# Moving the fourth gate step of each feed-forward's first chunk ahead of half of the operand building

## What is computed

```python
def rmsnorm(x, g):
    y = xf * lax.rsqrt(jnp.mean(xf * xf, axis=-1, keepdims=True) + EPS)
    return (y * g.astype(jnp.float32)).astype(x.dtype)

def swiglu(h, w_in, w_out):
    a, b = jnp.split(h @ w_in, 2, axis=-1)
    return (jax.nn.silu(a) * b) @ w_out
...
x = x + 0.5 * swiglu(rmsnorm(x, norm_ffn1[l]), ffn1_w_in[l], ffn1_w_out[l])
m, k, v, lf, s_fin = token_mix(...)
x = x + m
x = x + 0.5 * swiglu(rmsnorm(x, norm_ffn2[l]), ffn2_w_in[l], ffn2_w_out[l])
```

## Time and profile before

| | |
|---|---|
| median of 3 runs | 1251.35 us |
| the profiled execution, device time | 1252.58 us |
| its span | 1250.7 us |
| PE busy | 1210.6 us, 97% |
| DVE busy | 819.7 us, 66% |
| ACT busy | 572.0 us, 46% |
| POOL busy | 106.0 us, 8% |
| mean granted clock of TensorE | 0.994 |
| w_out loads of the first chunks, issue to landing | 2.9 us for 256 KB |

### The profile page before, as it was taken

The page is one execution under the profiler, slowest core; times in us unless marked ns, Lnnn a source line. Parts: engine busy times, 40 slices in busy tenths (PEclk is TensorE's granted clock), DMA queues, the critical chain, the costliest instruction groups (busy, mean ns, idle before and its releaser), DMA issues.

```text
span 1250.7 us, 29938 instructions
## 1 busy us (share of the span) xinstructions
PE 1210.6 (97%) x12005; PEld 1129.6 (90%) x12005; DVE 819.7 (66%) x1557; ACT 572.0 (46%) x1047; POOL 106.0 (8%) x247
## 2 busy tenths in 40 slices
PE   9999999999999999998978999999999999999998
PEld 8999999999999999996656666599989999999998
DVE  6799848838956423336756566654679839847954
ACT  6454424514534211535866776743345424524534
POOL 1000000000005000000222522214000000000000
PEclk9999999999999999999989999999999999999999
DMA  8133333233324343344798999723123332333322
GB/s 208 39 96 102 110 93 102 85 101 85 94 93 129 107 135 92 107 170 154 245 366 301 347 353 343 241 69 95 58 84 102 92 111 80 93 99 102 93 77 72
DMA packets 187145, 172.79 MB, mean 138 GB/s; under 512 B 11890, under 2 KB 149651, under 8 KB 187027
## 3 DMA queue, kind: packets, MB, share of 16 engines
q1 hardware_dynamic: 185858, 167.47, 42.5%
q0 software_dynamic: 1104, 3.67, 0.8%
q10 hardware_dynamic: 64, 0.02, 0.0%
HBM read 162.19 MB, written 8.93 MB: 137 GB/s over the span
## 4 chain that ended last, share of the span: by engine, by line
PE 82%; DVE 9%; issue 3%; ACT 3%; DMA 2%; SPq 0%; ACTq 0%; DVEq 0%; POOLq 0%
PE ps L2221 40%; PE ps L2359 28%; PE ps L1038 2%; PE ps L1123 2%; PE ps L1138 2%; PE ps L963 1%; DVE z_lo L2849 1%; PE ps L1003 1%; DMA d_keys<-in_cache_k 1%; PE ps L983 1%; DVE b_lo L2818 1%; PE ps L801 1%; ACT d_keysT L1383 1%; DVE z_sum L2826 0%; DMA d_log_f<-in_cache_logf,page_ids 0%
## 5 line engine op out<-in xcount | busy, mean ns | idle before, releaser
L2359 PE MATMUL ps<-b_lo,z_hi 128*128 128x272 f32 x1008 | 292.1, 290 | 0.0
L2359 PE MATMUL ps<-b_hi,z_hi 128*128 128x272 f32 x1008 | 290.8, 288 | 1.0 <-ACT z_kept L2566 1.0
L2359 PE MATMUL ps<-b_hi,z_lo 128*128 128x272 f32 x1008 | 290.9, 289 | 0.0
L2491 ACT ACTIVATE w_hi<-w_raw 128x2048 fp32r<-128x2048 f32 (+2 forms) x56 | 90.0, 1608 | 234.2 <-PE ps L2221 234.2
L2359 PEld LDWEIGHTS ps<-b_hi,z_hi 128*128 128x128 f32 x1008 | 190.0, 188 | 1.4 <-issue 1.4
L2359 PEld LDWEIGHTS ps<-b_hi,z_lo 128*128 128x128 f32 x1008 | 189.7, 188 | 0.0
L2359 PEld LDWEIGHTS ps<-b_lo,z_hi 128*128 128x128 f32 x1008 | 189.3, 188 | 0.0
L2221 PE MATMUL ps<-g_hi,w_hi 128*128 128x272 f32 x704 | 148.6, 290 | 6.6 <-DVE g_lo L2794 3.5
L2221 PE MATMUL ps<-n_hi,w_hi 128*128 128x272 f32 x704 | 148.9, 289 | 1.9 <-issue 1.0
L2221 PE MATMUL ps<-n_hi,w_lo 128*128 128x272 f32 x704 | 148.3, 288 | 0.0
L2221 PE MATMUL ps<-g_hi,w_lo 128*128 128x272 f32 x704 | 148.2, 289 | 0.0
(11 more groups left out here) (398 smaller groups left out, 1952.1 us busy)
## 6 DMA issues: line engine op xcount, KB each, us to landing
w_raw<-in_ffn_w_in SPq DMA_DIRECT2D x87, 512.0 KB, 5.0
d_keys<-in_cache_k SPq DMA_DIRECT2D x128, 256.0 KB, 5.3
d_values<-in_cache_v SPq DMA_DIRECT2D x124, 256.0 KB, 6.2
w_raw<-in_ffn_w_out SPq DMA_DIRECT2D x48, 384.0 KB, 3.6
w_raw<-in_w_in_mix SPq DMA_DIRECT2D x28, 512.0 KB, 4.8
w_raw<-in_ffn_w_out SPq DMA_DIRECT2D x16, 256.0 KB, 2.9
w_raw<-in_w_out_mix SPq DMA_DIRECT2D x8, 512.0 KB, 4.7
suffix_scratch<-d_log_f_sums SPq DMA_DIRECT2D x32, 64.0 KB, 2.1
```

The source lines that it names most:

```text
L2359: mm = pe.matmul(bank(out), w[j][:, a, k * P:(k + 1) * P], x, start=(k == 0 and n_pass == 0 and not more), stop=(k == KB - 1 and n_pass == ...
L2491: nc.scalar.activation(w_hi[j][:, 0:kt * UC], w_raw[j][:, 0:kt * UC], ACT.Copy).then_inc(w_hi_ready, 1)
```

## The change

The changed kernel has three edits. The first is in DVE's list of the first chunk: the building of B21 and B22 is cut in two halves of two instructions, and the fourth gate step stands between them. The second is in that gate step alone: the low part of A1's weight is written after `g_lo` and not before `ffn_gated`. The third is in PE's output units: the last two K tiles are taken one after the other, each with a wait of its own.

```diff
@@ unit
                 if x_wait is not None:
-                    order = [(t, k) for ks in (range(kt - 2), range(kt - 2, kt)) for t in range(2) for k in ks]
+                    order = [(t, k) for ks in (range(kt - 2), (kt - 2,), (kt - 1,)) for t in range(2) for k in ks]
@@ g_wait
-                        if k == 0 or k == kt - 2:
-                            pe.wait_ge(g_ready, done - 2 if k == 0 else done)
+                        if k == 0 or k >= kt - 2:
+                            pe.wait_ge(g_ready, done - 2 if k == 0 else done - (kt - 1 - k))
@@ gate_step of the vector block
-            def gate_step(pair, j, q, f, tile, next_kt, stage=None):
+            def gate_step(pair, j, q, f, tile, next_kt, stage=None, late_split=False):
...
-                split_lo(pair + 1, j, next_kt)
+                if not late_split:
+                    split_lo(pair + 1, j, next_kt)
...
                 nc.vector.tensor_tensor(lo, g_f[:, :, :], hi.bitcast(F32), ALU.subtract).then_inc(g_ready, 1)
+                if late_split:
+                    split_lo(pair + 1, j, next_kt)
@@ ffn of the vector block
                         gate_step(p0 + 1, 0, q0 + 2, f, 2, kt)
-                        build_full(f, norm, range(KB, KD))
-                        gate_step(p0 + 1, 1, q0 + 3, f, 3, kt)
+                        build_full(f, norm, range(KB, KB + 2))
+                        gate_step(p0 + 1, 1, q0 + 3, f, 3, kt, late_split=True)
+                        build_full(f, norm, range(KB + 2, KD))
                         build_sum(f, U1, b_full(f, B11), b_12[:, :, :], ALU.subtract)
```

## The result

The changed kernel is slower. In two comparisons, each against runs of the kernel before on the same chips, it took 1263.09 us (6 runs, 1258.26 to 1265.84) and 1261.02 us (6 runs, 1258.69 to 1265.35). The ratios are 1.0084 with a 95% interval of 1.0064 to 1.0103, and 1.0067 with 1.0045 to 1.0089, so it is 8 to 11 us slower. Forecast were 6.4 us and at most 9. The direction, the place and the length of DVE's list were right. The price of the slow clock was put too low, 3.0 us where it took 3.9 to 4.7 in two traces, and a third place, the last chunk of the first feed-forward, was not in the sum.

The account below looks back on a forecast made before the run. The prediction took DVE's list between `g_lo` and B0's low part as the bound: 1252.58 + 3.4 (list) + 3.0 (clock) = 1259.0 us against the profiled execution, median 1257.7, range 1254.0 to 1260.5.

Parts of the forecast that it names:

- What bounds the kernel: Ahead of B0, DVE's list from `g_lo` to the weight's low part sets its start; 0.26 us slack in first feed-forward.
- What edits 1 and 2 win: In the fourth gate step `g_lo` starts 0.92 us sooner in the first feed-forward, 0.71 in the second.
- What they cost: On DVE, `g_lo` to first sum grows from 0.64 to 3.27 us; sums start 1.71 and 1.92 us later.
- Edit 3 at nothing, and the stalls gathered into one: Added K tile waits cost nothing; PE's stall leaves A0, giving one gap of about 5 us ahead of B0 per feed-forward.
- Sum without the clock: At DVE's addition behind B0: +1.47 us in the first feed-forward, +1.92 in the second, together +3.4.
- The clock: During B0 the clock falls after both gathered gaps, 1.5 us each, +3.0; bounds nothing to 4.6 us each.
- In the later chunks ... PE does not stand at the last K tiles, so the order there changes nothing: In later chunks and first units with `x_in`, the new K tile order changes no time.
- the sign that all behind B0's addition would be later by one constant amount: Expected in the trace if right: everything from B0's addition on shifts later by one constant amount.
- the queue alone: DVE's list slips 3.4 us, clock holds or falls at one gap: 1254.7, or 1256.2 with one fall; chance 0.27.
- the exchange: Three instructions fit where DVE would wait anyway, the stall moves from A0 to B0: 1251.3; chance 0.04.
- the faster case: B0's low part does not decide B0's start, A0's stalls and slow clock are won, 5.0 us: 1246.3; chance 0.03.
- the slower case: Both gaps make the clock low for longer, 2.5 to 4.6 us each: 1259.7 to 1263.9; chance 0.08.

Follow-up runs that it names:

- the run with the gap filled: Changed kernel plus 36 matmuls with unread results at the end of A1 in both first chunks, output loop written out: 1256.51 us, ratio 1.0019.
- the run with the page sums late: Changed kernel with DVE's sums over the gathered values moved behind A1's weight in the first feed-forward's last chunk: 1260.07 us, ratio 1.0067.
- the run that had 0.2 and 0.4 us of list and lost 4.4: Changed kernel without the first edit, all four builds ahead of the fourth gate step again: 1256.82 us, ratio 1.0035.

## Why the prediction was wrong, point by point

- *What bounds the kernel:* right. In the changed kernel B0's low part set B0's start in both feed-forwards (before, PE ran from A0's gap into the first B0 without a pause, by the small slack that the prediction names); a longer list lost time, a shorter one won it.
- *What edits 1 and 2 win:* right, 0.9 and 0.7 us at `g_lo`. In the first feed-forward it starts 3.1 us after `ffn_a` (68.49 - 65.34) where it took 3.8 (69.17 - 65.33), and `ffn_a` itself waits for PE now and not for the builds; in the second the same 3.8 became 3.1.
- *What they cost:* right. 3.28 us from `g_lo` to the first sum against 3.27.
- *Edit 3 at nothing, and the stalls gathered into one:* the gap was forecast at about 5 us and measured at 5.15 and 4.94. That gathering has no price of its own was wrong: the run with edit 3 alone is 1.0023 of before.
- *Sum without the clock:* right. +3.4; 3.0 in the run with the gap filled, 3.4 with B0 started 0.34 us behind its low part as the sum has it.
- *The clock:* the step that failed. "I take a fall at both, 1.5 us each" carried the size of a fall after a gap of 1.88 us over to gaps of 5 us. The falls came at both. But of the six gaps of 4.94 to 5.15 us (the two traces and that of the run with the page sums late) five were followed by a low level of 6.8 us that began inside the gap, and one by 3.4 us. In the first trace B0 took 2.1 and 2.6 us longer, in the second 1.4 and 2.5: 4.7 and 3.9 us where the sum had 3.0. The case of longer falls, "2.5 to 4.6 us each", was named and given only 0.08.
- *"In the later chunks ... PE does not stand at the last K tiles, so the order there changes nothing":* true of the K tiles. But the gap at the gather was there before the change, its length varies from execution to execution, and I did not put it into the range. In the first trace that stretch carries 4.1 of 13.1 us. With it fell the sign that all behind B0's addition would be later by one constant amount.
- With 3.4 for the list, 3.9 to 4.7 for the clock and 0.2 for the first B0's later start the sum is 7.5 to 8.3 us, which is the second comparison (8.4 us by its ratio). The first, with 10.5 by its ratio, has 2 us more. That some of this is the gather is argued from one trace; the run that took the gather out of the way did not lower the median, so it stays open.
- The rivals: the queue alone and the exchange fell with the run that had 0.2 and 0.4 us of list and lost 4.4; the faster case fell with the changed kernel's gap ahead of B0; the slower case has the time right (1259.7 to 1263.9), but of its 2.5 to 4.6 us a gap only the second feed-forward reached the lower end (2.6 and 2.5), and in the first trace the gather made up the difference.

## What to carry to other kernels

Ask of every gap of PE what the next thing is that it will wait for: a stall that is removed ahead of a fixed later time is only moved, and if it joins another gap it can cost more than both did. Shorten the list of the engine that PE will wait for next before, or together with, taking away the wait in front of it: the same two edits lost 4 us with the list as it was and won 4 in the same two stretches (5 to 6 by the medians) with the short one. Idle time of the helping engine ahead of a step is where work for the list behind it should go.

## What the runs showed of the hardware

How often the clock fell against how long PE had stood, over all gaps of PE above 1 us ahead of or inside an output unit, in all fourteen traces of this study, the one of before among them: of 15 gaps of up to 2.07 us one was followed by a fall, of 8 gaps between 2.56 and 2.95 us five, of 10 gaps from 3.44 to 5.15 us all ten. This counts output units alone. In the mixing layer, where PE has many short gaps besides, the clock fell as well around gaps of 2.01, 2.08 and 2.19 us and held after one of 2.48 (the kernel before, at 628.01). So in these traces no length between 1.9 and 3 us tells by itself what follows. A fall is not a fixed cost: the low level lasted about 3.4 us or about 6.8 us, and it cost B0 between 1.4 and 2.6 us. The landing of one and the same gather of 128 rows took between 5.9 and 7.9 us in the fourteen traced executions.
